# First keys and queries of attention loaded at the end of the projections, other traffic held back, and some slab copies on VectorE

## The reference, cut to what matters

```python
o1 = attend(dq[:, :, :, 0], dk[:, :, :, 0], dv, sc)
o2 = attend(dq[:, :, :, 1], dk[:, :, :, 1], dv, sc)
o_diff = rmsnorm(o1 - lam.astype(o2.dtype) * o2, subln_g) * (1.0 - lam_init)
o_gqa = attend(gq, gk, gv, sc)
```

## Time and profile before

| | |
|---|---|
| median of 3 runs | 2223.13 us (2220.74 to 2223.78) |
| the profiled execution's own time | 2224.07 us |
| its span, first to last instruction | 2222.0 us |
| mean granted TensorE clock | 0.961 |
| PE busy | 1999.5 us (90%) |
| DVE busy | 1546.1 us (70%) |
| ACT busy | 1378.3 us (62%) |
| POOL busy | 938.0 us (42%) |
| HBM read, written | 360.83 MB, 96.26 MB |

### The profile page before, as it was taken

How to read it: one execution, slowest core, us unless ns; L and a number is a source line. 1 busy time by engine, 2 the same in 40 slices (tenths; PEclk the granted TensorE clock), 3 DMA queues, 4 the chain that set the end, 5 groups by cost and what they waited for, 6 DMA issues and landing times.

```text
span 2222.0 us, 36247 instructions
## 1 busy us (share of the span) xinstructions
PE 1999.5 (90%) x9592; PEld 1490.4 (67%) x9592; DVE 1546.1 (70%) x2158; ACT 1378.3 (62%) x2000; POOL 938.0 (42%) x869
## 2 busy tenths in 40 slices
PE   5899995688988889879989999999999999999993
PEld 2776664555555555467646888888877888888881
DVE  3752373585336743246446999999988999999995
ACT  2422121465656566522336999899878998999982
POOL 1010011651115511006453666656665666666663
PEclk7999998799999999888999999999999999999997
DMA  7464345711122121248536999799999977789967
GB/s 260 138 185 134 108 133 175 215 39 41 36 53 44 29 44 36 81 160 157 131 90 251 307 352 315 230 297 300 353 330 351 347 241 224 229 245 353 303 152 255
DMA packets 162651, 429.16 MB, mean 193 GB/s; under 512 B 26993, under 2 KB 82033, under 8 KB 137889
## 3 DMA queue, kind: packets, MB, share of 16 engines
q1 hardware_dynamic: 92818, 294.36, 36.6%
q0 software_dynamic: 60048, 116.89, 23.6%
q10 hardware_dynamic: 9712, 16.99, 2.6%
HBM read 360.83 MB, written 96.26 MB: 206 GB/s over the span
## 4 chain that ended last, share of the span: by engine, by line
PE 45%; DMA 6%; DVE 2%; issue 2%; ACT 1%; SPq 1%; ACTq 0%; POOL 0%; DVEq 0%; POOLq 0%
PE ps_d L2031 11%; PE ps_r L2014 8%; PE ps_r L2016 7%; PE ps_r L2015 7%; DMA w_experts<-in_w_exp_down 5%; PE ps_y L1937 4%; PE ps_y L2004 3%; PE ps_g L1954 2%; PE ps_d L1971 1%; PE ps_g L2038 1%; PE ps_t L1917 0%; DMA y_tiles_odd<-y_scratch 0%; DMA o_in<-o_scratch 0%; DVE x_row L1672 0%; DMA y_scratch<-e_y,e_target_index 0%
## 5 line engine op out<-in xcount | busy, mean ns | idle before, releaser
L1782 DVE TENSOR_TENSOR w_gate_up_low<-w_experts,w_gate_up_high 128x1024 fp32r<-128x1024 f32 x416 | 489.2, 1217 | 18.5 <-ACT w_gate_up_high L1551 18.4
L1551 ACT ACTIVATE w_gate_up_high<-w_experts 128x1024 fp32r x416 | 416.5, 1049 | 31.9 <-SPq L1309 16.9
L940 DVE TENSOR_REDUCE neg_max<-ps_scores 128x1 f32<-128x1280 f32 x128 | 190.2, 1489 | 232.9 <-PE ps_scores L1025 232.5
L2014 PE MATMUL ps_r<-w_gate_up_high,gatheredT_high 128*128 128x512 f32 x832 | 336.0, 404 | 3.0 <-DVE gatheredT_low L1788 2.7
L1440 POOL DMA_INDIRECT y_scratch<-e_y,e_target_index x104 | 288.6, 2775 | 108.0 <-POOL e_target_index L1436 93.5
L2016 PE MATMUL ps_r<-w_gate_up_high,gatheredT_low 128*128 128x512 f32 x832 | 326.8, 393 | 0.0
L2015 PE MATMUL ps_r<-w_gate_up_low,gatheredT_high 128*128 128x512 f32 x832 | 324.6, 390 | 0.0
L1817 DVE TENSOR_TENSOR w_down_low<-w_experts,w_down_high 128x2048 fp32r<-128x2048 f32 x103 | 236.1, 2293 | 43.9 <-ACT w_down_high L1576 43.4
L1426 POOL DMA_INDIRECT gathered<-h_scratch,e_gather_index x106 | 194.2, 1832 | 95.9 <-POOL e_gather_index L1423 90.8
L1025 PE MATMUL ps_scores<-k_high_low,q_high 128*128 128x512 f32 (+1 forms) x384 | 166.4, 433 | 58.8 <-DMA k_high_low<-k_scratch 29.5
L1576 ACT ACTIVATE w_down_high<-w_experts 128x2048 fp32r x103 | 197.9, 1922 | 32.9 <-issue 32.9
(11 more groups left out here) (278 smaller groups left out, 3937.0 us busy)
## 6 DMA issues: line engine op xcount, KB each, us to landing
w_experts<-in_w_exp_gate SPq DMA_DIRECT2D x64, 1024.0 KB, 9.5
w_experts<-in_w_exp_up SPq DMA_DIRECT2D x64, 1024.0 KB, 13.8
w_experts<-in_w_exp_down SPq DMA_DIRECT2D x64, 1024.0 KB, 17.4
w_mod_later<-in_w_mod ACTq DMA_DIRECT2D x32, 512.0 KB, 3.8
w_mod_first<-in_w_mod SPq DMA_DIRECT2D x4, 2048.0 KB, 15.5
w_in_raw<-in_w_in SPq DMA_DIRECT2D x32, 256.0 KB, 3.5
k_high_low<-k_scratch POOLq DMA_DIRECT2D x10, 640.0 KB, 8.8
values<-in_tokens SPq DMA_DIRECT2D x10, 512.0 KB, 11.3
```

The source lines that it names most:

```text
L1551: act.activation(split_slice(eH, j), raw_slice(ring, slot, j), ACT.Copy).then_inc(X["wH"], 1)
L1782: nc.vector.tensor_tensor(split_slice(eL, j), raw_slice(ring, slot, j), split_slice(eH, j).bitcast(F32), ALU.subtract).then_inc(X["wL"], 1)
L2014: nc.tensor.matmul(psR[:], xH[:, k], eH[:, k], start=(k == 0), stop=False)
```

## The change: what it does

Three things. (1) The buffers of unit 0's queries (`q_first`) and of key heads 0 and 1 (`k_first`) are laid over `wl`, `raw` and `cp` of the projections, and live through both blocks, as do the semaphores `s_q` and `s_k`. GpSimd loads them at the end of `front`: the two keys when all weights have been split, all modulation products made and the last partial product spread, the queries when the stores of tiles 2 to 5 have landed. `attention` then begins with key 2, unit 1's queries, key 3. (2) SyncE issues the copies, the zeros and the output weights only when all ten keys have landed. (3) In GQA units slabs 1, 5 and 8 are copied by VectorE and not by ScalarE, with a semaphore of their own (`s_evd`); `tr` and `pv` wait for whichever engine copies the slab. `first` in `attention` is renamed `row0`.

```diff
+def load_queries(eng, s_q, dst, q_d, h0, nh, at, w):
+    for part in range(2):
+        for r in range(2):
+            eng.dma_start(dst[r * HD:(r + 1) * HD, part, 0:nh * w].rearrange("p (c n) -> p c n", n=w),
+                          q_d[part, h0:h0 + nh, :, at:at + w].rearrange("c d n -> d c n")).then_inc(s_q, 16)
+
+def load_key(eng, s_k, dst, k_d, hd):
+    eng.dma_start(dst, k_d[hd].rearrange("e d n -> (e d) n")).then_inc(s_k[hd // 2], 16)
...
-        raw = b.sb(ph, "w_in_raw", [P, RAW, 512])
+        zone = (16 + 25) * 1024
+        wl = b.at("w_mod_later", [P, 2, QK, MC], F32, zone)
+        raw = b.at("w_in_raw", [P, RAW, 512], F32, zone + 8 * 1024)
+        cp = b.at("mod_part", [P, MC], F32, zone + 16 * 1024)
...
+            qf, kf = first
+            pool.wait_ge(s_wl, len(CH) * KD)
+            pool.wait_ge(s_mt, NM)
+            pool.wait_ge(s_mm, EARLY + 4 * (NM - EARLY))
+            for hd in range(2):
+                load_key(pool, s_k, kf[:, hd], k_d, hd)
+            ready = turned.index(first_of[-1] + 4)
+            for u in range(2):
+                pool.wait_ge(s_st[u], stored(u, ready))
+            load_queries(pool, s_q[0], qf, q_d, 0, 2, 0, 512)
...
+    def by_dve(g):
+        return units[g // KT_N][0] == "g" and g % KT_N in (1, 5, 8)
+
+    def wait_out(eng, g):
+        if by_dve(g):
+            eng.wait_ge(s_evd, sum(1 for h in range(g + 1) if by_dve(h)))
+        else:
+            eng.wait_ge(s_ev, sum(1 for h in range(g + 1) if not by_dve(h)))
...
-        qh = b.sb(ph, "q_high", [P, 2, 1024], F32R)
-        ql = b.sb(ph, "q_low", [P, 2, 1024], F32R)
-        k2 = b.sb(ph, "k_high_low", [P, NKH, KEYS], F32R)
+        qf, kf = first
+        qs = b.sb(ph, "q_second", [P, 2, 1024], F32R)
+        k2 = b.sb(ph, "k_high_low", [P, NKH - 2, KEYS], F32R)
...
             sp.dma_start(sg[:], a["subln_g"].broadcast_to([P, DIFF_V])).then_inc(s_g, 16)
+            for w in s_k:
+                sp.wait_ge(w, 32)
             sp.dma_start(rows_d, rows[0:1].rearrange("p r n -> p (r n)")).then_inc(s_later, 16)
...
-            sp.wait_ge(s_q[1], 64)
             sp.dma_start(wa[:], a["w_out"][0, 0:wa.shape[1] * P, :].rearrange("(k p) n -> p k n", p=P)).then_inc(s_later, 16)
...
-            load_k(0)
-            load_q(0)
-            load_k(1)
-            load_k(2)
-            load_k(3)
+            load_key(pool, s_k, key(2), k_d, 2)
             load_q(1)
+            load_key(pool, s_k, key(3), k_d, 3)
...
+            def out_p(u, kt):
+                g = u * KT_N + kt
+                if not by_dve(g):
+                    return
+                dve.wait_ge(s_tr, g + 1)
+                if g >= KEEP:
+                    dve.wait_ge(s_pv, g - KEEP + 1)
+                nc.vector.tensor_copy(pd[:, g % KEEP], pT(u, kt)).then_inc(s_evd, 1)
...
                 for kt in range(KT_N):
+                    out_p(u, kt)
                     if kt in at:
                         rowmax(u + 1, at[kt])
...
-                pe.wait_ge(s_ev, g + 1)
+                if kind == "g":
+                    wait_out(pe, g - 1)
+                wait_out(pe, g)
```

More of the change, by code:

```diff
@@ L84, with front @@
 A2, B2, G1, G2 = range(4)
-def front(b, a, ident, rows, nlam, mhalf, vv, q_d, k_d):
+def load_queries(eng, s_q, dst, q_d, h0, nh, at, w):
[5 more added lines that the diff above has]
+    eng.dma_start(dst, k_d[hd].rearrange("e d n -> (e d) n")).then_inc(s_k[hd // 2], 16)
+def front(b, a, ident, rows, nlam, mhalf, vv, first, s_q, s_k, q_d, k_d):
     nc = b.nc
@@ L680, in _, with attention @@
                     mod_products(wl[:, i % 2], h * QK, QK, h < 2, h >= 2, s_mm)
-def attention(b, a, ident, rows, nlam, mhalf, moe, wa, vv, q_d, k_d, o_d, rows_d, slot_d, y2_d):
+def attention(b, a, ident, rows, nlam, mhalf, moe, wa, vv, first, s_q, s_k, q_d, k_d, o_d, rows_d, slot_d, y2_d):
     nc = b.nc
@@ L698, in n_rows @@
         return 8 if units[u][0] == "d" else 4
-    first = [sum(n_rows(v) for v in range(u)) for u in range(NU + 1)]
+    row0 = [sum(n_rows(v) for v in range(u)) for u in range(NU + 1)]
     n_diff = [sum(1 for v in range(u) if units[v][0] == "d") for u in range(NU + 1)]
@@ L790, in attention, with key @@
         S = psS[:].rearrange("p b n -> p (b n)")
+        def key(hd):
+            return kf[:, hd] if hd < 2 else k2[:, hd - 2]
         def pT(u, kt):
@@ L867, in _ @@
             for hd in range(4, NKH):
-                load_k(hd)
+                load_key(pool, s_k, key(hd), k_d, hd)
             nc.gpsimd.memset(ones[:], 1.0)
@@ L882, in exp @@
             def exp(u, r):
-                n, row = first[u] + r, r % 2
+                n, row = row0[u] + r, r % 2
                 act.wait_ge(s_m, n + 1)
@@ L937, in rowmax @@
             def rowmax(u, r):
-                n = first[u] + r
+                n = row0[u] + r
                 dve.wait_ge(s_s, n + 1)
@@ L1023, in qk @@
                         pe.wait_ge(s_e, n)
-                    for part in (qh, ql):
-                        last = nc.tensor.matmul(S[:, base + at:base + at + w], part[:, u % 2, cols], k2[:, kv_head(u, r), at:at + w],
-                                                start=(part is qh), stop=(part is ql))
+                    for part in range(2):
+                        last = nc.tensor.matmul(S[:, base + at:base + at + w], (qf, qs)[u % 2][:, part, cols], key(kv_head(u, r))[:, at:at + w],
+                                                start=(part == 0), stop=(part == 1))
                 last.then_inc(s_s, 1)
@@ L2129, in program @@
             vv = b.sb(kv, "values", [P, KT_N, VW])
-            front(b, a, ident, rows, nlam, mhalf, vv, q_d, k_d)
+            first = (b.sb(kv, "q_first", [P, 2, 1024], F32R), b.sb(kv, "k_first", [P, 2, KEYS], F32R))
+            s_q = [b.sem(top, f"q_loaded{j}") for j in range(2)]
+            s_k = [b.sem(top, f"k_loaded{j}") for j in range(5)]
+            front(b, a, ident, rows, nlam, mhalf, vv, first, s_q, s_k, q_d, k_d)
             K = 1024
@@ L2134, in program @@
                    b.at("first_rows", [P, E], F32, 203 * K + 256), token)
-            attention(b, a, ident, rows, nlam, mhalf, moe, wa, vv, q_d, k_d, o_d, rows_d, slot_d, y_d[1])
+            attention(b, a, ident, rows, nlam, mhalf, moe, wa, vv, first, s_q, s_k, q_d, k_d, o_d, rows_d, slot_d, y_d[1])
             tail(b, a, ident, rows, mhalf, moe, wa, p8, s_slots, s_w, o_d, x1_d, h2_d, y_d, slot_d, rows_d, out)
```

22 lines of the change are left out of this document (8 added, 14 removed).

## The result

The changed kernel takes 2189.97 us (median of 4 runs, 2186.32 to 2190.55), the kernel before on the same chip 2222.33 us (4 runs, 2220.74 to 2223.78): a ratio of 0.985 with an interval of 0.983 to 0.987. The forecast was 2185, 2177 to 2200. The profiled execution took 2190.17 us, its span 2188.4, against 2222.0 before.

| stretch | before | after | gain |
|---|---|---|---|
| to the last turn of a projection tile | 366.58 | 363.90 | 2.68 |
| from there to the first score matmul | 30.08 | 5.79 | 24.29 |
| first score to the end of unit 0 (`oT_head` written) | 53.15 | 57.08 | -3.93 |
| units 1 to 23 | 476.74 | 462.45 | 14.29 |
| behind attention | 1295.45 | 1299.18 | -3.73 |

What follows compares the result with a forecast made beforehand. TensorE was taken as the bound, except at the seam, where it waits for first keys and queries. Seam 24.3 plus copies 13.8 make 38.1 us off 2224.07, giving 2186.0; the median runs 0.94 lower, so 2185, range 2177 to 2200.

Steps and rivals of the forecast that it cites:

- The seam: Between projections and attention: early keys and queries let the first score matmul start at 372.4, not 396.66, gaining 24.3 us.
- the late-data rival: At the seam: queries land late (up to 381.4) or early loads hold up stores; 2194 or 2197 us, chance 0.12.
- the bound of 15.3: At the seam: the gain if early queries land as late as the slowest query load, starting scores at 381.4.
- The copies: In the 16 GQA units: VectorE copying slabs 1, 5 and 8 gains 13.8 us, 0.91 per plain unit.
- The two rivals in which VectorE's order gives the gain back: In GQA units: copies only move the hole (2199 us, chance 0.14), or copies delay row maxima (2232 us, chance 0.03).
- the one unit where the prediction had seen it: Second single-bank unit ahead of the second differential group: a row maximum ahead of slab 5's copy costs 1.1 us.
- Traffic held back: SyncE's copies, zeros and output weights wait for ten keys, then run 30 us in the first differential units; effect zero.
- Unit 0: Attention's first unit: same clock at the start as before and later work simply 24.3 us earlier; effect 0.
- From there the old order runs 24.3 us earlier: Attention after unit 1's loads, judged hidden with 8 us to spare: everything keeps its order, 24.3 us earlier.
- if it stays down for all eight rows: Unit 0's score rows: a clock staying low for all eight would lose some 4 us; taken as 0.
- the 1.3 us that a kept clock would have added: First two score rows: a shorter pause keeping the clock up would gain up to 1.3 us more; taken as 0.
- a sign of being wrong: Behind attention: the prediction is wrong if the stage of the experts changes its length; the same length was forecast.

Runs made afterwards that it cites:

- the copies alone: The kernel before with only part 3 (VectorE copies slabs 1, 5 and 8 of each GQA unit): 2208.1 us, ratio 0.992.
- the gain's scaling first: VectorE's wait for `sub_gain` and its scaling left ahead of the first row maximum, as in the changed kernel: 2189.97 us, repeated 2193.1 us, both ratio 0.985.
- the 30 matmuls: The changed kernel plus 30 128x512 matmuls, results unread, in TensorE's pauses at the projections' end: 2193.1 us, ratio 0.985; also combined with other edits.
- the gain late: The changed kernel with VectorE's `sub_gain` wait and scaling moved behind unit 1's first row maximum: 2182.1 us, again 2188.2 us (ratio 0.983); also combined with other edits.

## Why the prediction was right, and where it was off

**The seam (24.3 us forecast).** Right in place and size: 24.29. From the last turn to the first score it took 5.67 to 6.06 us in all eleven profiles with the early loads and 30.08 to 30.42 in the three without. Queries issued at 353.21 and keys at 337.04 were there, so neither the late-data rival nor the bound of 15.3 came into play. The first score came at 369.69 and not at 372.4 because the projections had ended 2.7 us earlier in that execution; they ended anywhere from 363.77 to 366.81 in fourteen profiles, with and without the change.

**The copies (13.8 us).** Right: 14.3, by unit 0.98 where 0.91 was said, 1.3 where 1.29, 1.89 where 1.8, -1.07 where -1.1, 1.38 where 0.91 + 0.5. These add up to 14.6; the thirteenth unit took 0.33 of them back, which the copies alone don't explain (its length varies by itself, see the end). The 0.07 us in a plain unit are the slab's own time, taken as 0.46: from slab 2 to the score row behind slab 3 it was 1.78 us before (550.35 to 552.13) and is 0.80 now (525.95 to 526.75). The two rivals in which VectorE's order gives the gain back fell with them, apart from the one unit where the prediction had seen it. A copy takes 687 ns. That a VectorE copy in a two-port mode holds up GpSimd (the Trainium skill, SBUF - State Buffer, Who interferes with whom) was not to be seen here: four query issues take 2.45 us in the plain unit with a copy in their middle (the POOL row above), and before the change the same four, without one, took 2.45 as well. The Trainium skill's other page (VectorE: DVE Perf Modes, Mode 2x_2P) asks for a source in SBUF in that mode, which these copies don't have; the trace agrees with that. No run here has a copy from SBUF beside GpSimd's issues, so the first rule itself is untested.

**Traffic held back (0).** Right in its size: nobody waits, and with the traffic let go at once TensorE waits 1.45 us for a key, which no unit's length shows. The picture is another than the one forecast. DMA is quiet from 380 to 394.5 (0.01) not because all ten keys are in but because GpSimd mixes before it issues keys 4 to 9; these and unit 2's queries fill the engines from 394.5 (1.07), and the block of held-back traffic, some 30 us as forecast, comes behind 409.13 (0.97). So the change moves the zeros and copies, some 5 MB, out of a stretch in which the DMA engines then lie idle for 14.5 us; it cost nothing that these runs show.

**Unit 0 (0).** This is the step that failed, in two places. "From there the old order runs 24.3 us earlier" passed over VectorE, whose first row maximum stands behind a wait for a DMA issued after the seam. That wait was much the same before (3.1 us from the DMA's issue, 3.6 now); 24 us of TensorE's idleness covered it. The prediction's own question, where a stall goes and what is late next, was answered for keys and queries alone. The delay itself is 1.45 us. The other place is the clock, taken as the same as before, with a loss of 4 us "if it stays down for all eight rows" as the bound. What was lost, 3.93 us, has the size of that bound, but by luck: the clock did not stay down for all rows (0.74 from 375 to 395), and part of the loss lies behind the eight rows. In six profiles with the gain's scaling first (that with the 30 matmuls among them) unit 0 took 55.2 to 57.6 us, in the five with it late 52.1 to 54.2, in the three with the old loads 51.9 to 53.2; the mean granted clock of the unit was 0.75 to 0.84, 0.82 to 0.87 and 0.86. So moving two small instructions and their wait gave back some 3.7 us (the means are 56.8 and 53.1): by the table in the experiments half of it ahead of the first turn, where the delay's own 1.4 are (and in two of the five late profiles the 30 matmuls' 1.2), half behind it, at a higher clock (0.88 to 0.98 for 0.81 to 0.89). Why a late start should leave TensorE at the lower clock 30 us on isn't shown: the runs show that the two go together, with overlap, and that a full clock at the seam (the 30 matmuls) does not prevent it.

The Trainium skill (TensorE: Matmul & The Clock Gate, HAM oscillation) has new work start cold behind a wait. The trace agrees, for pauses far shorter than the 29 us of before: 0.55 behind the pause of 4.98 us, and 0.50 behind one of 4.04 us, although the clock had been 1.00 up to it. By that rule the 1.3 us that a kept clock would have added don't come, and they didn't: with the gain late the first row maximum stands 2.51 us behind the first score, as before the change, and 1.43 us where the 30 matmuls held the clock up.

**Behind attention (0).** The prediction had named a changed length of the experts' stage as a sign of being wrong. It was 3.7 us longer here, which needs no cause in the change: 1295.45 and 1300.20 in the kernel before, 1295.70 to 1303.70 in twelve others. The means are 1297.4 in three profiles with the old loads and 1299.1 in eleven with the early ones, so a share of up to some 2 us isn't excluded. The fifth term of the table is the spread of that stretch, as the first is of the projections; in this pair they cancel to 1.1 us.

So of 38.1 us forecast, 33.9 came in the profiled execution (2224.07 to 2190.17): 24.3 and 14.3 as said, 3.9 lost in unit 0, 1.1 lost between two stretches that vary by themselves, and 0.3 gained in what lies around the span. By the medians it was 32.4 us; the medians of one kernel on four occasions lay 6 us apart, so that last difference tells nothing. Attention ended 37.3 us earlier (38 forecast), 2.7 of which are the projections' own spread. The median is 5.0 us above the forecast; 3.9 of that are unit 0's loss, which no term of the sum had and the range allowed for as the clock's.

## What to carry to other kernels

When a long wait goes, list on every engine what stands ahead of its first useful instruction, the small set-up steps and their DMAs too: each of them was hidden by the wait and none is now. An engine that takes copies in a strict order gains only at the slabs whose buffer somebody waits for; one copy of three did all the good in a plain unit, and the other two paid in some units and cost in one. Traffic held back until loads have landed also waits for whoever issues these loads: look at what that engine does first. Don't pay for a warm TensorE ahead of a wait: remove the wait first, and see whether anything is left.

## What the runs showed of the hardware

- The clock fell inside attention too. The thirteenth unit took 26.2 us in the five profiles in which the stretch from 629 to 712 us had a granted clock of 1.00 (one of them the kernel before), and 27.1 to 28.4 us in the other nine, with 0.96 to 0.98 and the dip at changing places. Up to 2.2 us of 24 units' time are decided there. The five are four of the five profiles with the gain late, one of the three with the old loads, and none of the six with the gain first; whether the edit has a part in that isn't shown, and no run here was made for it.
- The same 111 matmuls of unit 0, from its first turn to its end, took 25.13 us at a granted clock of 0.96 to 0.99, 26.5 to 26.6 at 0.88 to 0.90, and 28.3 to 28.6 at 0.81 to 0.82, in fourteen profiles of eleven kernels.
- A copy of 128x512 words from the accumulators takes VectorE 687 ns and ScalarE 596 (page of after), so moving one costs 0.09 us more where it lies on the path: the wait at a turn was 0.78 us for the one and 0.69 for the other.
